# Sums of squares with the square tile as weight, centred norms shifted in two steps, buffers at multiples of 64 bytes, four weights asked for first

## The reference, cut to what matters

```python
def layer_norm(x, g, b):
    mu = jnp.mean(x, axis=-1, keepdims=True)
    var = jnp.mean(jnp.square(x - mu), axis=-1, keepdims=True)
    return (x - mu) * lax.rsqrt(var + LN_EPS) * g + b

for l in range(DEPTH):                       # first block, DEPTH = 2
    h = hybrid_mixer(x, ...)
    x = layer_norm(ALPHA * x + h, ln1_g[l], ln1_b[l])
    h = memory_cross_attention(x, mem, x_wq[l], x_wkv[l], x_wo[l])
    x = layer_norm(ALPHA * x + h, ln2_g[l], ln2_b[l])
    h = conv_ffn(x, f_w_up[l], f_conv_k[l], f_conv_b[l], f_w_down[l])
    x = layer_norm(ALPHA * x + h, ln3_g[l], ln3_b[l])

def sandwich(x, c_act, sublayer, g_pre, g_post, w_mod, b_mod):   # second block, four times
    shift, scale, gate = jnp.split(c_act @ w_mod + b_mod, 3, axis=-1)
    h = rms_norm_2(x, g_pre) * (1 + scale[:, None]) + shift[:, None]
    return x + gate[:, None] * rms_norm_2(sublayer(h), g_post)
```

## Time and profile before

| | |
|---|---|
| median of 3 runs | 3758.27 us (3756.89 to 3759.4) |
| profiled execution | 3756.42 us, span 3754.6 us |
| PE busy | 3562.8 us, 95% of the span |
| DVE, ACT, POOL busy | 1604.7, 1013.9, 2072.2 us |
| granted TensorE clock, mean | 0.971 |
| chain that ended last | PE 87%, DVE 6%, ACT 4% |

### The profile page before, as it was taken

The page is one execution under the profiler, slowest core; times in us unless marked ns, Lnnn a source line. Parts: engine busy times, 40 slices in busy tenths (PEclk is TensorE's granted clock), DMA queues, the critical chain, the costliest instruction groups (busy, mean ns, idle before and its releaser), DMA issues.

```text
span 3754.6 us, 44932 instructions
## 1 busy us (share of the span) xinstructions
PE 3562.8 (95%) x17537; PEld 2765.0 (74%) x17537; DVE 1604.7 (43%) x2437; ACT 1013.9 (27%) x1955; POOL 2072.2 (55%) x2138
## 2 busy tenths in 40 slices
PE   8999988999999999889998999997999899989998
PEld 6777776888777777768886666775888677668886
DVE  3564435755336553367553544334322233233222
ACT  2344224212123441332112454333111133211111
POOL 5444563767554446557774554442666544447664
PEclk9999999999999999999998999998999999989999
DMA  4222222665221213236642222221333222123332
GB/s 137 62 63 61 86 86 72 197 184 174 84 73 54 68 43 112 73 114 186 188 128 68 68 67 68 73 59 52 104 95 93 85 69 61 57 62 90 96 91 73
DMA packets 578795, 345.20 MB, mean 92 GB/s; under 512 B 16032, under 2 KB 562073, under 8 KB 578585
## 3 DMA queue, kind: packets, MB, share of 16 engines
q1 hardware_dynamic: 574637, 337.34, 30.8%
q10 hardware_dynamic: 3947, 4.99, 0.4%
HBM read 340.14 MB, written 2.14 MB: 91 GB/s over the span
## 4 chain that ended last, share of the span: by engine, by line
PE 87%; DVE 6%; ACT 4%; issue 1%; DMA 1%; POOL 0%; SPq 0%; ACTq 0%; DVEq 0%
PE gemm L220 24%; PE gemm L223 23%; PE gemm L226 23%; PE scores L300 6%; PE outs L300 6%; PE gemm L255 1%; PE scores L1455 1%; PE gemm L256 1%; PE gemm L257 1%; DMA w_raw<-in_w_in 1%; ACT tiles L633 1%; DVE x_t L1110 0%; DVE tiles L1107 0%; DVE scales L702 0%; ACT tiles L605 0%
## 5 line engine op out<-in xcount | busy, mean ns | idle before, releaser
L199 POOL CAST w_high<-w_raw 128x512 fp32r<-128x512 f32 (+1 forms) x1067 | 698.8, 655 | 1565.8 <-PE gemm L226 1176.8
L201 POOL TENSOR_TENSOR w_low<-w_raw,w_high 128x512 fp32r<-128x512 f32 (+1 forms) x1067 | 1385.2, 1298 | 85.4
L220 PE MATMUL gemm<-x_high,w_high 128*128 128x512 f32 x2584 | 714.0, 398 | 21.5 <-POOL w_high L199 5.4
L223 PE MATMUL gemm<-x_low,w_high 128*128 128x512 f32 x2584 | 694.5, 391 | 0.0
L226 PE MATMUL gemm<-x_high,w_low 128*128 128x512 f32 x2584 | 691.7, 390 | 0.0
L220 PEld LDWEIGHTS gemm<-x_high,w_high 128*128 128x128 f32 x2584 | 474.3, 188 | 129.0 <-issue 18.4
L223 PEld LDWEIGHTS gemm<-x_low,w_high 128*128 128x128 f32 x2584 | 486.0, 188 | 105.0
L226 PEld LDWEIGHTS gemm<-x_high,w_low 128*128 128x128 f32 x2584 | 485.1, 188 | 103.4
L220 PE MATMUL gemm<-split_tiles,w_high 128*128 128x512 f32 (+1 forms) x1456 | 396.3, 392 | 8.4 <-DVE tiles L1545 2.4
L223 PE MATMUL gemm<-split_tiles,w_high 128*128 128x512 f32 (+1 forms) x1456 | 388.2, 387 | 0.0
L226 PE MATMUL gemm<-split_tiles,w_low 128*128 128x512 f32 (+1 forms) x1456 | 386.9, 386 | 0.0
(11 more groups left out here) (342 smaller groups left out, 3605.3 us busy)
## 6 DMA issues: line engine op xcount, KB each, us to landing
w_raw<-in_mlp_w SPq DMA_DIRECT2D x112, 512.0 KB, 4.0
w_raw<-in_mod_w SPq DMA_DIRECT2D x96, 512.0 KB, 3.7
w_raw<-in_w_in SPq DMA_DIRECT2D x88, 512.0 KB, 3.7
w_raw<-in_f_w_up SPq DMA_DIRECT2D x88, 512.0 KB, 4.9
w_raw<-in_e_w_in SPq DMA_DIRECT2D x48, 512.0 KB, 3.9
w_raw<-in_f_w_down SPq DMA_DIRECT2D x32, 512.0 KB, 4.1
w_raw<-in_o_w_in SPq DMA_DIRECT2D x30, 512.0 KB, 3.8
w_raw<-in_w_branch SPq DMA_DIRECT2D x48, 256.0 KB, 2.6
```

What stands on the lines that cost most here:

```text
L199: me.pool.tensor_copy(WH[:, h, 0:n], W32[:, s, c0:c0 + n]).then_inc(sem["w_rounded"], 1)
L201: me.pool.tensor_tensor(WL[:, h, 0:n], W32[:, s, c0:c0 + n], WH[:, h, 0:n].bitcast(F32), ALU.subtract).then_inc(sem["w_split"], 1)
L220: me.pe.matmul(o, WH[:, h, (k - k0) * cols:(k - k0 + 1) * cols], src(k)[0], start=begin and k == 0, stop=False)
L223: me.pe.matmul(o, WH[:, h, (k - k0) * cols:(k - k0 + 1) * cols], src(k)[1], start=False, stop=False)
```

## The change

**Sums of squares.** The square tile is now the weight (128 tokens at a time, a 128x128 weight) and one column of `mean` moves, so that the sum of token t of block q stands in partition t, column q: four columns instead of four strips of 128. A matmul of 4 columns by a zero (`sums_begun`) opens the accumulation. The scales are then 128x4; the spread takes a broadcast column of them as weight and the identity as moving operand. This holds for the RMS norms, the centred norms and the hand-over.

**Centred norms.** The mean of the first 6 tiles (5 in ln2), scaled up to a mean of all, is made inside unit 6 (behind unit 5 in ln2). DVE subtracts it from these tiles, and from the later ones as they come; ACT squares them at once; PE sums the squares of the first 6 inside unit 7 (those of the first 5 behind unit 7 in ln2). Behind the last unit comes the mean of what is left, in two forms: per token as four one-column matmuls (to correct the variance) and over all partitions as one of 512 columns; DVE subtracts it from the eight tiles again (`centre_tile`), three ahead of the scaling. In ln1 the fifth key unit moves ahead between the mix units, and three are left as fills.

**Buffers.** `work`, `split_tiles` and `plain_tiles` are allocated behind `mats`: work now begins at byte 155264 and split_tiles at 171648, both multiples of 64.

**Start.** SP asks for the first four weights right behind x; ACT asks for the identity alone; the other constants, c, the mask and the nine parts of tables go through SP behind the four weights. `layer_columns`, the Silu and the wait for the constants stand behind the first unit pair.

```diff
+        T2 = sb("work", [P, 8, S])
+        with nc.sbuf_tensor("split_tiles", [P, RT, S], F32R) as R:
+            pass
+        RF = sb("plain_tiles", [P, RT, S])
...
-        T2 = sb("work", [P, 8, S])
...
+        def norm_square(j):
+            return T[:, 16 + j if j < 4 else 5 + j, :]
+        def part_moved(me, j, after):
+            moved = me.tick("dve_step")
+            if me.dve:
+                me.dve.wait_ge(sem["pe_step"], me.part_mean)
+                me.dve.wait_ge(sem["dve_step"], after)
+                me.dve.tensor_tensor(X[:, j, :], X[:, j, :], O[:, 0, :], ALU.subtract).then_inc(sem["dve_step"], 1)
+            me.square_made[j] = me.tick("act_step")
+            if me.act:
+                me.act.wait_ge(sem["dve_step"], moved)
+                me.act.activation(norm_square(j), X[:, j, :], ACT.Square).then_inc(sem["act_step"], 1)
+            return moved
+        def mean_part(me, j, added, first):
...
+            moved = part_moved(me, j, added)
+            if j > first:
+                me.rest_total = me.tick("dve_step")
+                if me.dve:
+                    me.dve.wait_ge(sem["dve_step"], moved)
+                    me.dve.tensor_tensor(total, X[:, first, :] if j == first + 1 else total,
                                          X[:, j, :], ALU.add).then_inc(sem["dve_step"], 1)
...
+        def first_mean(me, first):
+            me.part_mean = me.tick("pe_step")
+            if me.pe:
+                me.pe.wait_ge(sem["dve_step"], me.part_total)
+                mm(me, O[:, 0, :], M["mean"], T[:, 13, :]).then_inc(sem["pe_step"], 1)
+            if me.act:
+                me.act.activation(st[:, 60:61], zero[:], ACT.Sqrt)
+            me.square_made = {}
+            for j in range(first):
+                part_moved(me, j, me.part_added)
+        def square_sums(me, first, last):
+            for j in range(first, last):
+                if me.pe:
+                    me.pe.wait_ge(sem["act_step"], me.square_made[j])
+                    if j == 0:
+                        sums_begun(me)
+                    for q in range(4):
+                        done = mm(me, O[:, 1, q:q + 1], norm_square(j)[:, q * P:(q + 1) * P], M["mean"][:, 0:1],
+                                  False, j == KD - 1 and q == 3)
...
+        def sums_begun(me):
+            mm(me, O[:, 1, 0:4], M["ident"], zero[:].broadcast_to([P, 4]), True, False)
...
+                    if i == 0:
+                        sums_begun(me)
                     for q in range(4):
-                        last = mm(me, O[32 * q:32 * q + 32, 1, 0:P], M["mean"][:, 0:32],
-                                  T[:, 16 + i % 4, q * P:(q + 1) * P], i == 0, i == KD - 1)
+                        last = mm(me, O[:, 1, q:q + 1], T[:, 16 + i % 4, q * P:(q + 1) * P], M["mean"][:, 0:1],
+                                  False, i == KD - 1 and q == 3)
                     last.then_inc(sem["pe_step"], 1)
...
+        def centred_norm(me, g, b, first, fills, hand_over=False):
+            t, s_ = T2, scale_rows[:, 0:4]
+            total = T[:, 13, :]
             fills[0]()
...
+            shift, squared = me.tick("pe_step"), me.tick("act_step")
             if me.pe:
+                me.pe.wait_ge(sem["dve_step"], me.rest_total)
+                for q in range(4):
+                    last = mm(me, Q[:, 2, q:q + 1], total[:, q * P:(q + 1) * P], M["mean"][:, 0:1])
                 last.then_inc(sem["pe_step"], 1)
+            if me.act:
+                me.act.wait_ge(sem["pe_step"], shift)
+                me.act.activation(s_, Q[:, 2, 0:4], ACT.Square).then_inc(sem["act_step"], 1)
+            square_sums(me, first, KD)
+            centre = me.tick("pe_step")
+            if me.pe:
+                mm(me, Q[:, 3, :], M["mean"], total).then_inc(sem["pe_step"], 1)
             fills[1]()
-            spread = scale_out(me, summed, 1.0, 1e-5)
+            spread_var, root, rec = me.tick("dve_step"), me.tick("act_step"), me.tick("dve_step")
+            if me.dve:
+                me.dve.wait_ge(sem["act_step"], squared)
+                me.dve.wait_ge(sem["pe_step"], me.squares_summed)
+                me.dve.scalar_tensor_tensor(s_, O[:, 1, 0:4], 1e-5, s_, ALU.add,
+                                            ALU.subtract).then_inc(sem["dve_step"], 1)
+            if me.act:
+                me.act.wait_ge(sem["dve_step"], spread_var)
+                me.act.activation(s_, s_, ACT.Sqrt).then_inc(sem["act_step"], 1)
+            if me.dve:
+                me.dve.wait_ge(sem["act_step"], root)
+                me.dve.reciprocal(s_, s_).then_inc(sem["dve_step"], 1)
+            centred = {}
+            def centre_tile(j):
+                centred[j] = me.tick("dve_step")
+                if me.dve:
+                    if j == 0:
+                        me.dve.wait_ge(sem["pe_step"], centre)
+                    me.dve.tensor_tensor(X[:, j, :], X[:, j, :], Q[:, 3, :], ALU.subtract).then_inc(sem["dve_step"], 1)
+            for j in range(AHEAD):
+                centre_tile(j)
+            spread = me.tick("pe_step")
+            if me.pe:
+                me.pe.wait_ge(sem["dve_step"], rec)
+                for q in range(4):
+                    last = mm(me, O[:, 0, q * P:(q + 1) * P], s_[:, q:q + 1].broadcast_to([P, P]), M["ident"])
+                last.then_inc(sem["pe_step"], 1)
             fills[2]()
...
                 if j < KD:
                     scaled[j] = me.tick("dve_step")
                     if me.dve:
+                        me.dve.wait_ge(sem["dve_step"], centred[j])
                         me.dve.scalar_tensor_tensor(t[:, j, :], X[:, j, :], g[:, j:j + 1], O[:, 0, :], ALU.mult,
                                                     ALU.mult).then_inc(sem["dve_step"], 1)
+                    if j + AHEAD < KD:
+                        centre_tile(j + AHEAD)
...
-            s_ = scale_rows[:]
+            s_ = scale_rows[:, 0:4]
             moved, root, rec, spread = me.tick("dve_step"), me.tick("act_step"), me.tick("dve_step"), me.tick("pe_step")
             if me.dve:
                 me.dve.wait_ge(sem["pe_step"], summed)
-                me.dve.tensor_scalar(s_, O[:, 1, 0:P], 1024.0 * ratio, 1024.0 * eps, ALU.mult,
+                me.dve.tensor_scalar(s_, O[:, 1, 0:4], ratio, eps, ALU.mult,
                                      ALU.add).then_inc(sem["dve_step"], 1)
             if me.act:
                 me.act.wait_ge(sem["dve_step"], moved)
...
-                    last = mm(me, O[:, 0, q * P:(q + 1) * P], M[f"row{q}"], s_)
+                    last = mm(me, O[:, 0, q * P:(q + 1) * P], s_[:, q:q + 1].broadcast_to([P, P]), M["ident"])
...
-            centred_norm(me, c["ln1_g"], c["ln1_b"], (lambda: keys(4, 5), lambda: keys(5, 6), lambda: keys(6, 8)))
+            centred_norm(me, c["ln1_g"], c["ln1_b"], 6, (lambda: keys(5, 6), lambda: keys(6, 7), lambda: keys(7, 8)))
...
-            centred_norm(me, c["ln2_g"], c["ln2_b"], (lambda: None, lambda: None, lambda: None))
+                if j == 5:
+                    first_mean(me, 5)
+                mean_part(me, j, added, 5)
+            square_sums(me, 0, 5)
+            centred_norm(me, c["ln2_g"], c["ln2_b"], 5, (lambda: None, lambda: None, lambda: None))
 
...
-            order = [j // 3 if j % 3 == 2 else None for j in range(12)]
+            order = [None, None, 0, None, 1, None, 2, None, 3, None, 4, None, None]
...
-                    done = unit(me, wcols(a["w_mix_out"], l, 0, KD, j * P), KD, xs, bank, ready=made if j == 0 else None)
+                    done = unit(me, wcols(a["w_mix_out"], l, 0, KD, j * P), KD, xs, bank, ready=made if j == 0 else None,
+                                between={6: lambda: first_mean(me, 6), 7: lambda: square_sums(me, 0, 6)}.get(j))
...
-                me.act.dma_start(MAT[:], a["mats"]).then_inc(sem["mats_landed"], 16)
-                with nc.allow_non_contiguous_dma(reason="one column of eight"):
-                    me.act.dma_start(c_act, a["c_2"][0].rearrange("(t p) -> p t", p=P)).then_inc(sem["c_landed"], 16)
-                me.act.dma_start(mask[:], a["band"]).then_inc(sem["c_landed"], 16)
-            for part in range(9):
-                layer_rows(me, 0, me.act, part, None)
+                me.act.dma_start(MAT[:, 0, :], a["mats"][:, 0, :]).then_inc(sem["ident_landed"], 16)
+            me.early = [issue_fetch(me, wcols(a["w_in"], 0, 0, KD, n * P), KD * P, P) for n in (16, 17, 18, 19)]
+            for part in (2, 3, 4, 5, 6, 7, 8, 0, 1):
+                if part == 0:
+                    if me.sp:
+                        me.sp.dma_start(MAT[:, 1:len(CONSTS), :],
+                                        a["mats"][:, 1:len(CONSTS), :]).then_inc(sem["mats_landed"], 16)
+                        with nc.allow_non_contiguous_dma(reason="one column of eight"):
+                            me.sp.dma_start(c_act, a["c_2"][0].rearrange("(t p) -> p t", p=P)
```

(3 more changed lines are left out.)

106 lines of the change are left out of this document (53 added, 53 removed).

## The result

The changed kernel takes 3783.86 us (median of 4 runs, 3779.5 to 3790.9) against 3757.58 us of the kernel before beside it (3756.1 to 3759.4): a ratio of 1.0072, 95% interval 1.0054 to 1.0089, so 0.7% slower (26 us between the medians, 27 by the ratio). The forecast was 3768 (+0.25%), its range 3712 to 3800.

A forecast was written before the change was run, and what follows sets the result against it. PE was taken as the bound (87% of the span); -27 +12.3 -1.9 +8.7 -2.6 +8.5 +16.8 -5.5 = +9.3 gave 3765.7 us profiled, 3767.6 beside the median, range 3712 to 3800.

The forecast's parts named there:

- first case: The sum as worked out, clock falling to 1.2 GHz in one-column rows: 3767.6 us, own range 3750 to 3785; chance 0.60.
- the other rival (the clock holds): Weight loads keep the clock at the upper level in one-column rows: -49 us, 3709; chance 0.20.
- the third one: Rival that alignment does nothing: moved buffers change no cadence, the -27 is missing, 3795 us; chance 0.17.
- One of the signs: Sign of being right: granted clock near 0.5 in the 24 sums inside unit 7.
- aligned tiles: GEMM matmuls from split_tiles at multiples of 64 bytes gain 6.7 ns per 512 columns, 4032 matmuls: -27 us.
- sums of the second block and hand-over: Second-half sums: +12.3 in the GEMM flow, -1.9 smaller scales, +8.7 behind post norms, hand-over +2.3 and -1.0.
- start: First unit pair starts at 15.8 instead of 24.27; part given back for late tables and low clock: -5.5 us.
- centred norms: Two-step shift with one-column sums at low clock: ln1 -2.6, ln2 +8.5, ln3 and hand-over together +16.8 us.
- Sums between the units: Between GEMM units, one tile's sum costs 0.855 us on PE instead of 0.45, for 28 tiles: 11.4 us.
- Squares behind the post norm: Behind post norms, a tile's sum takes 1.7 us at 1.2 GHz and PE becomes the bound: +8.7 us for three.
- the 3.4 for the low clock in ln3: In ln3's flow, low clock over part of the one-column row and the matmuls behind it adds 3.4 us.
- the 12.9: In ln3 of layer 0, 12.9 us from the last gemm to the unit pair.

The follow-up runs named there:

- e1_align: The kernel before with only work, split_tiles and plain_tiles allocated behind mats, at multiples of 64 bytes; ratio 0.9952 to the kernel before.
- e2_rms: The kernel before with only the second block's and hand-over's sums of squares in one-column form; ratio 1.0061 to the kernel before.
- e5_start: The kernel before with the new start alone; ratio 0.9986 to the kernel before.
- e3_old_sums: The changed kernel with the sums turned back to 32-wide weights, 128 columns moving and scales of 128x128; ratio 0.9879 to the kernel before.
- e9_shift_alone: The kernel before with only the two-step shift of the centred norms, sums still 32-wide; ratio 0.9949 to the kernel before.
- e8_warm: e3_old_sums with square-tile weights and 128 moving columns behind post norms and at the hand-over, plus matmuls that make nothing where PE waits; ratio 0.9832 to the kernel before.
- e4_wide_moving: The changed kernel with each one-column sum moving 128 columns of mean and openers zeroing 512 columns; ratio 0.9963 to the kernel before.
- e11_best: e8_warm with layer_columns, Silu, sink operation and waits on constants behind the first four units and an earlier gelu table load; ratio 0.9851 to the kernel before.

## Why the forecast was right, and where it was off

The direction and the case were right: the clock fell in the one-column rows (first case), the other rival (the clock holds) did not happen in the changed kernel, and the addresses did work (the third one fell). The size was short: +9 was summed, +27 came (by the ratio), and 3784 us is only just inside the first case's own range, which ended at 3785. All four terms of the table missed to the same side, so nothing cancelled. One of the signs came only in part: in the 24 sums inside unit 7 the clock was to be near 0.5, and it is 1.00 for the first 3.1 us. Term by term:

| term | forecast | measured | by |
|---|---|---|---|
| aligned tiles | -27 | -18 (-13 to -23) | e1_align |
| sums of the second block and hand-over: 12.3 - 1.9 + 8.7 + 2.3 - 1.0 | +20.4 | +23 (18 to 28) | e2_rms |
| start | -5.5 | -5 (-2 to -9) | e5_start |
| centred norms: -2.6 + 8.5 + 16.8, less the hand-over's 1.3 | +21.4 | +27 (about 10 either way) | the rest |
| sum | +9.3 | +27 (20 to 33) | |

- **Aligned tiles** was the term most off, by 9 us. The mechanism was right, and so were the 6.7 ns in undisturbed stretches, but not over all 4032 matmuls. The groups by line and shape of before and e1_align show where the rest went: the three groups of 1328 from split_tiles are busy 1107.4 us before and 1084.8 after, 22.6 us less or 5.7 ns a matmul; the three groups of 128 matmuls with 256 columns rise by 1.2 us, where 1.3 were counted as a gain; and the three groups from x_high and x_low, which no edit touched, rise by 3.3 us. That makes the 18. The last part is a difference of 0.2% between two executions and may be chance. "Some 5% of it falls where PE waits anyway" was not the place.
- **Sums between the units**: 0.81 against the 0.855 forecast. **Squares behind the post norm**: 1.72 a tile against 1.7.
- **Centred norms.** ln2 came nearly as worked out (19.1 and 13.6 against 18.5 and 13.0), and so did ln1: 30.7 us from 531.90 to the end of the pair, 2.8 for the key unit moved ahead, and 0.9, 6.8 and 2.0 inside the flow are 43.2, forecast 42.0. ln3 didn't: in layer 0 the row inside unit 7 took 7.45 us (5.3 plus a part of 3.4 was the forecast), the 18 matmuls behind it 3.0 more than at full clock, and from the last gemm (1027.1) to the pair (1042.5) it is 15.4 us, not 12.9, since from 1030.02 on the whole chain ran at a granted clock of 0.50. The terms that were too small are the 3.4 for the low clock in ln3 and the 12.9: the forecast let a part of these rows run at the upper level.
- The rows of ln3 in layer 0 of the changed kernel, PE, on which the last point rests:

```profile
1012.69 7.45 PE L310 MATMUL outs<-mats,tiles 128*128 128x1 f32 x48
...
1020.00 2.05 PE L228 MATMUL gemm<-split_tiles,w_high 128*128 128x512 f32 x4
...
1030.02 1.87 PE L310 MATMUL scores<-mats,tiles 128*128 128x1 f32 x8 [2.79 <-DVE tiles L634]
...
1037.01 1.91 PE L310 MATMUL outs<-mats,scales 128*128 128x128 f32 x8
```

- **A price read too high.** The forecast took the 32-wide sum at 0.45 a tile, from one tile between two units. In a row of six it is 0.24 (e3_old_sums); the 0.45 holds the change from unit to sum and back. So the sum of the whole was not wrong by it, but the two parts of the centred norms were never seen apart: the two-step shift is worth -19 us (e9_shift_alone), and its one-column sums cost some 46, the 27 of the table less these -19. The prediction put them together as "added", and gave no version in which the shift pays.
- **The start** was right as a whole: pair at 16.5 for 15.8, 4.9 us ahead at the next unit, 3.3 after the clock had dipped.

## What to carry to other kernels

Weigh a small matmul by what it streams as well as by its loads: a long row of wide loads with a column behind each (24 here; four did not do it) costs its own time and then halves the clock of the first GEMM matmuls behind it; four narrow weights side by side are cheaper, and where PE waits anyway, matmuls that make nothing can pay for themselves (11 us here in a kernel of 3757, and 9 more in e8_warm). Start the moving operand of a 512-column matmul like these at a multiple of 64 bytes; 32 past it is the only other place that was tried. And when a change has several parts, price each with its own before and after: here two parts that gain 37 us and one that gains 5 were hidden by one that loses some 70.

## What was not expected of the hardware

- Two spacings of one shape, by start address: 226.7 ns at a multiple of 64 bytes, 233.3 ns at 32 past it, in both directions of the test. For 256 columns 118 and 120 ns were seen, and they do not follow the start of split_tiles.
- The clock at 0.50 with PE and its loads recorded busy 14.2 of 14.9 us (2642.37 to 2657.31), and at 1.00 with PE busy 9.7 of 11.5 us once 128 columns moved in place of one (2605.15 to 2616.69 of e4_wide_moving). The forecast had this from one short stretch of 32-wide sums at 0.51.
- Even in stretches that no edit touched, two executions differ by steps of 1.6 us where the clock dips in one and not in the other: from 1700 to 1710 us it is 0.83 in e11_best and 1.00 in e8_warm. A few such steps would make the 11 us between the shortest and the longest run of the changed kernel, though no run isolates that.
